# Cutting 1092 token columns as 512 + 512 + 68 in the dense products of a decoder-layer kernel

## Chip, cores and metric

One core of a Trainium2 chip. The metric is the device time in microseconds of one execution of the whole program, on inputs of fixed shape.

## What is computed

One layer of a hybrid decoder, on a prompt of 1024 tokens and on 8 sequences of 8 new tokens each, which makes 1088 tokens; all data is fp32. Cut to what matters:

```
def trunk_layer(x, ...):
    xn = rmsnorm(x, attn_norm_g)
    proj = xn @ w_in                                   # 1024 -> 3088
    gla_o  = gated linear attention, chunked           # 4 heads, 64/128
    diff_o = differential attention                    # 4 heads; 8 samples read a paged cache of 4096 tokens
    h = x + concat(norm(gla_o) * silu(gg), norm(diff_o)) @ w_out     # 1024 -> 1024
    hn = rmsnorm(h, ffn_norm_g)
    h = h + (silu(hn @ w_ffn_gate) * (hn @ w_ffn_up)) @ w_ffn_down   # 1024 -> 2816 -> 1024
    gate = sigmoid(rmsnorm(h, ple_norm_g) @ w_ple_gate)              # 1024 -> 1024
    return h + gate * (p @ w_ple_proj)                               # 256 -> 1024
```

## The kernel before

The activations stand transposed in SBUF: 128 features on the partitions, the tokens along the free dimension, `T = 3 * SPAN = 1092` columns (1088 tokens and four columns of padding, `SPAN = 364`). PSUM has 8 banks of 512 fp32 per partition. Two accumulators of three banks each, `dense[0]` (banks 0 to 2) and `dense[1]` (banks 3 to 5), take turns as the output of a dense product; two further banks, `misc`, take transposes and small products.

Every dense product is done by one helper, `product` (lines 143 to 156). It is given one tile of 128 output features and goes over the blocks of 128 input features (`ks`: 8 for an input width of 1024, 2 for an input width of 256). Weights and activations are each split into a high and a low part of type float32r (`whi`, `wlo`, `xhi`, `xlo`), and for each block three products are accumulated: high by high, high weight by low activation, low weight by high activation. Each of these three is cut along the token columns into three matmuls of 364 columns, `c` = 0, 1, 2, one to a bank (line 150). A matmul is at most 512 columns wide. Each of them is issued with a weight load of its own, although the three in a row use the same weights. After a block, `between` may put in other work of TensorE: transposes of an earlier tile (lines 435, 1832, 1854, 2319, 2329) or the sums of squares for the query and key norms (line 454).

The stages, in order of time:

- Input projection, line 425: 25 tiles of 8 blocks. ScalarE evacuates the accumulators (lines 367, 386, 392, 398, 404).
- Gated linear attention (lines 771 to 868), prompt attention (lines 1200 to 1224) and decode attention with its paged cache (lines 1448 to 1510). They don't call `product`. They hold plain fp32 matmuls and transposes of other shapes.
- Mixer output, line 1862: 8 tiles of 8 blocks; VectorE adds the result to h (line 1929).
- FFN, lines 2105 and 2114: 44 gate and up tiles of 8 blocks, scaled by VectorE (line 2146), and 11 times 8 down tiles of 2 blocks, added by VectorE (line 2167).
- Embedding, lines 2339 and 2348: 8 gate tiles of 8 blocks into `dense[0]` and 8 projection tiles of 2 blocks into `dense[1]`; VectorE evacuates both (lines 2402 and 2410). Line 2414 adds h.

Together 200 + 64 + 352 + 176 + 64 + 16 = 872 blocks.

The weights of a tile come by a DMA on SyncE's queue, GpSimd scales them by the norm's gain, ScalarE rounds them to the high part (`w_hi`, line 2051 in the FFN, 2283 in the embedding), and VectorE subtracts to get the low part (`w_lo`). All order between the engines is written out by hand with semaphores: TensorE waits for `w_lo` of the tile and for `evacuated` of the tile two before it (same accumulator), and counts up `product_done` with the tile's last matmul; the evacuating engine waits for that. The high part of a later tile waits for `product_done` too, as its buffer is reused.

The evacuations read an accumulator in its three spans, for which a view takes the first 364 of each bank's 512 elements, and `spans` (line 138) gives the SBUF side the same shape:

```
def spans(ap):
    return ap.rearrange("p (c n) -> p c n", n=SPAN)
...
dve.tensor_tensor(spans(m.h[:, n]), spans(m.h[:, n]), dense[n % 2][:, :, 0:SPAN], ALU.add
```

Of the kernel before, what the change touches and what calls it, by code (L numbers as in the profile page):

```python
# [15 lines left out]
ALU = mybir.AluOpType  # L16
ACT = mybir.ActivationFunctionType
# [8 lines left out]
SPAN = 364  # L26
T = 3 * SPAN
# [110 lines left out]
def spans(ap):  # L138

    return ap.rearrange("p (c n) -> p c n", n=SPAN)  # L140


def product(pe, out, whi, wlo, xhi, xlo, ks, between=()):

    for n, k in enumerate(ks):
        for w, x in ((whi, xhi), (whi, xlo), (wlo, xhi)):
            for c in range(3):
                ins = pe.matmul(out[:, c, 0:SPAN], w(k), x(k)[:, c * SPAN:c * SPAN + SPAN],  # L150
                                start=n == 0 and w is whi and x is xhi, stop=n == len(ks) - 1 and w is wlo)
        if n in dict(between):
            for work in dict(between)[n]:
                work()
    return ins


def input_projection(nc, io, m, ps, scr, sems):
# [21 lines left out]
    evacuated = sems("p1_evacuated")  # L180
# [15 lines left out]
    dense, misc = ps["dense"], ps["misc"]  # L196
# [22 lines left out]
    plan, n = {}, XT + 3 * 8  # L219
# [7 lines left out]
    with nc.Block() as block:  # L227
# [101 lines left out]
        def _(act):  # L329
# [17 lines left out]
            def hi(s, slot, first=False):  # L347
                act.wait_ge(w_scaled, s + 1)
                if not first:
                    act.wait_ge(product_done, s - 1)  # L350
                act.activation(m.whi[:, slot], m.raw[:, slot], ACT.Copy).then_inc(w_hi, 1)

            for g, (c0, cn) in enumerate(CHUNKS):
# [3 lines left out]
                for k in range(KT):  # L357
                    n = g * KT + k
# [3 lines left out]
            with act.Fori(0, 4) as i:  # L362
                for u in range(2):
                    s = 2 * i + u
                    act.wait_ge(product_done, s + 1)
                    act.wait_ge(filled, s * 3 + (XT - 3))
                    act.activation(spans(m.f[:, u]), dense[u][:, :, 0:SPAN], ACT.Copy).then_inc(evacuated, 1)
                    hi(s + 2, u)

            for s in range(8, 17):  # L370
                u, r = s % 2, s - 8
                if s >= 9:

                    v = 1 - u
                    act.wait_ge(taken, plan["ss", s - 1] + 3)
                    act.activation(m.rs[:, v], m.rs[:, v], ACT.Ln, scale=1.0 / DK, bias=m.eps[:, :]
                                   ).then_inc(ln_done, 1)
                    act.wait_ge(ln_done, s - 8)
                    act.activation(m.rs[:, v], m.rs[:, v], ACT.Exp, scale=-0.5).then_inc(rs_done, 1)
                act.wait_ge(product_done, s + 1)  # L380
                if s < 16:
                    if r < 2:
                        act.wait_ge(filled, XT + 3 * (s - 2) + 3)
                    else:
                        act.wait_ge(normed, r - 1)
                    act.activation(spans(m.f[:, u]), dense[u][:, :, 0:SPAN], ACT.Copy).then_inc(evacuated, 1)
                    act.wait_ge(evacuated, s + 1)
                    if r >= 2:
                        act.wait_ge(filled, plan["ss", s - 2] + 3)
                    act.activation(m.sq[:, u], m.f[:, u], ACT.Square).then_inc(squared, 1)  # L390
                else:
                    act.activation(spans(m.g[:, 0, :]), dense[0][:, :, 0:SPAN], ACT.Copy).then_inc(evacuated, 1)
                hi(s + 2, u)
            with act.Fori(0, 3) as i:
                for v in range(2):
                    s = 2 * i + (17 + v)
                    act.wait_ge(product_done, s + 1)
                    act.activation(m.g[:, bass.ds(2 * i + (1 + v), 1), :].rearrange("p o (c n) -> p (o c) n", n=SPAN),
                                   dense[1 - v][:, :, 0:SPAN], ACT.Copy).then_inc(evacuated, 1)
                    hi(s + 2, 1 - v)  # L400
            act.wait_ge(roped, 8)
            for s in (23, 24):
                act.wait_ge(product_done, s + 1)
                act.activation(spans(m.g[:, s - 16, :]), dense[s % 2][:, :, 0:SPAN], ACT.Copy).then_inc(evacuated, 1)

        @block.tensor
        def _(pe):
# [1317 lines left out]
def mixer(nc, io, m, ps, scr, sems):  # L1725
# [5 lines left out]
    s = {n: sems("p5_" + n) for n in names.split()}  # L1731
# [6 lines left out]
    dense, misc = ps["dense"], ps["misc"]  # L1738
# [7 lines left out]
    with nc.Block() as block:  # L1746
# [134 lines left out]
        def _(dve):  # L1881
# [29 lines left out]
            v = last.rearrange("p (h v) -> p h v", v=DV)  # L1911
# [14 lines left out]

            def evac(n):
                dve.wait_ge(s["product_done"], n + 1)
                dve.tensor_tensor(spans(m.h[:, n]), spans(m.h[:, n]), dense[n % 2][:, :, 0:SPAN], ALU.add
                                  ).then_inc(s["evacuated"], 1)  # L1930

            take_x(1, 16)
            evac(0)
            lo(2, 0)
            take_x(17, 24)
# [11 lines left out]
def ffn(nc, io, m, ps, scr, sems):  # L1947
# [11 lines left out]
    s = {n: sems("p6_" + n) for n in names.split()}  # L1959
# [4 lines left out]
    dense = ps["dense"]  # L1964
# [26 lines left out]
    with nc.Block() as block:  # L1991
# [142 lines left out]
        def _(dve):  # L2134
# [8 lines left out]
            def scaled(x, dst, bank):  # L2143

                dve.wait_ge(s["product_done"], x + 1)
                dve.tensor_tensor(spans(dst), dense[bank][:, :, 0:SPAN], spans(m.rb[:, :]), ALU.mult  # L2146
                                  ).then_inc(s["evacuated"], 1)

            def gate(j, f, x):
# [14 lines left out]

            def add(x, n):
                dve.wait_ge(s["product_done"], x + (n + 1))
                dve.tensor_tensor(spans(m.h[:, n]), spans(m.h[:, n]), dense[n % 2][:, :, 0:SPAN], ALU.add  # L2167
                                  ).then_inc(s["evacuated"], 1)

            lo(0, 0, 0)  # L2170
# [43 lines left out]
def embedding(nc, io, m, ps, scr, sems):  # L2214
# [5 lines left out]
    s = {n: sems("p7_" + n) for n in names.split()}  # L2220
    w_in = [sems(f"p7_w_in{u}") for u in range(2)]
    stored = [sems(f"p7_stored{u}") for u in range(2)]
    dense, misc = ps["dense"], ps["misc"]
# [6 lines left out]
    with nc.Block() as block:  # L2230
# [132 lines left out]
        def _(dve):  # L2363
# [34 lines left out]
            def scaled(n):  # L2398
                if not (isinstance(n, int) and n == 0):
                    dve.wait_ge(s["gated"], n)  # L2400
                dve.wait_ge(s["gate_done"], n + 1)
                dve.tensor_tensor(spans(m.gt), dense[0][:, :, 0:SPAN], spans(m.rb[:, :]), ALU.mult
                                  ).then_inc(s["gate_scaled"], 1)

            def result(n, u):
                dve.wait_ge(s["sigmoid_done"], n + 1)
                dve.wait_ge(s["proj_done"], n + 1)
                if not (isinstance(n, int) and n < 2):
                    dve.wait_ge(s["filled"], n * 3 + (PT - 3))
                dve.tensor_tensor(spans(m.gp[:, u]), spans(m.gt), dense[1][:, :, 0:SPAN], ALU.mult  # L2410
                                  ).then_inc(s["gated"], 1)
                dve.wait_ge(s["gated"], n + 1)
                h = m.h[:, bass.ds(n, 1), :].rearrange("p o t -> p (o t)")
                dve.tensor_tensor(m.gp[:, u], m.gp[:, u], h, ALU.add).then_inc(s["y_done"], 1)  # L2414
# [9 lines left out]
            with dve.Fori(0, 2) as i:  # L2424
                for u in range(2):
                    n = 2 * i + (2 + u)
# [112 lines left out]
```

## Time and profile before

| | us |
|---|---|
| timed executions, two | 2159.78 and 2168.81 |
| their median | 2164.3 |
| span of the profiled execution, first to last instruction | 2161.1 |
| TensorE busy with matmuls in the span | 1927.8 (89%) |
| TensorE busy with weight loads | 1743.4 (81%) |
| VectorE busy | 972.4 (45%) |
| ScalarE busy | 605.6 (28%) |
| GpSimd busy | 404.4 (19%) |

PE is TensorE's matmul side and PEld its weight loads, which overlap matmuls; DVE is VectorE, ACT ScalarE, POOL GpSimd, SP SyncE. The duration in a matmul's row runs from its start to the end of its results, so that the rows of neighbours overlap; the time between the starts of two matmuls is shorter than a row. Of a group of n records in a timeline the printed time runs from the first start to the last end. For the profiled execution only its span is known; what lies around it isn't listed separately.

### The profile page before, as it was taken

Reading aid. Unit: us, or ns where it says so; the run is one execution under the profiler, and the core shown is the slowest. Engines: PE = TensorE matmul, PEld = TensorE weight load, DVE = VectorE, ACT = ScalarE, POOL = GpSimd, SP = SyncE. Lnnn points to the kernel's source line nnn. Section 1 sums busy time; section 2 is a strip of 40 time slices with the busy share of each in tenths; the row PEclk is TensorE's granted clock in tenths of the full one; section 3 lists DMA queues with packets and bytes.
Section 4 is the critical chain, followed back from the end, with each engine's and each line's share of the span. In section 5 each row is a group of like instructions: output and inputs, shape, how many; then the busy total and the mean of one; then the engine's idle time right before and its main releaser. Section 6 shows DMA issues by size and latency. Waiting matters only on the chain. (4 is left out here: it accounts for less than half of the span.)

```text
span 2161.1 us, 36230 instructions
## 1 busy us (share of the span) xinstructions
PE 1927.8 (89%) x13348; PEld 1743.4 (81%) x13348; DVE 972.4 (45%) x1364; ACT 605.6 (28%) x1011; POOL 404.4 (19%) x398
## 2 busy tenths in 40 slices
PE   5999998556887789888789899999999999999798
PEld 4999998543555566656589899999999999999798
DVE  4224611784666545555533523433343334335543
ACT  4113312531444444444432211111111111112420
POOL 1112321331000234343311100110111011102210
PEclk9999999785878999999999999999999999999899
DMA  4323521005300799999721111111111111110221
GB/s 130 102 80 101 154 70 50 21 3 192 113 1 0 247 378 387 387 387 387 250 61 40 49 49 39 49 40 50 39 48 42 49 40 39 50 50 20 66 75 42
DMA packets 187844, 236.56 MB, mean 109 GB/s; under 512 B 12994, under 2 KB 127635, under 8 KB 187731
## 3 DMA queue, kind: packets, MB, share of 16 engines
q1 hardware_dynamic: 167250, 167.81, 24.3%
q0 software_dynamic: 20480, 67.13, 8.4%
q8 instruction: 85, 1.39, 0.3%
q14 instruction: 29, 0.23, 0.0%
HBM read 213.49 MB, written 16.92 MB: 107 GB/s over the span
## 5 line engine op out<-in xcount | busy, mean ns | idle before, releaser
L150 PE MATMUL psum<-h_hi,w_hi 128*128 128x364 f32 x1248 | 279.2, 332 | 2.5 <-issue 2.5
L150 PE MATMUL psum<-h_lo,w_hi 128*128 128x364 f32 x1248 | 276.6, 330 | 0.0
L150 PE MATMUL psum<-h_hi,w_lo 128*128 128x364 f32 x1248 | 275.4, 329 | 0.0
L2051 ACT ACTIVATE w_hi<-w_raw 128x1024 fp32r<-128x1024 f32 x66 | 68.9, 1060 | 584.4 <-PE psum L150 566.1
L150 PEld LDWEIGHTS psum<-h_hi,w_hi 128*128 128x128 f32 x1248 | 215.6, 189 | 4.6 <-issue 4.4
L150 PEld LDWEIGHTS psum<-h_lo,w_hi 128*128 128x128 f32 x1248 | 217.5, 189 | 0.0
L150 PEld LDWEIGHTS psum<-h_hi,w_lo 128*128 128x128 f32 x1248 | 217.1, 189 | 0.0
L2027 POOL TENSOR_TENSOR w_raw<-w_raw,gains 128x1024 f32<-128x1024 f32 x42 | 80.3, 1913 | 652.2 <-DMA w_raw<-in_w_ffn_gate 352.2
L150 PE MATMUL psum<-x_hi,w_hi 128*128 128x364 f32 x792 | 187.6, 345 | 11.1 <-DVE x_lo L1884 7.3
L1081 POOL DMA_DIRECT2D dec_v<-in_cache_v x256 | 138.0, 539 | 266.4 <-issue 263.3
L150 PE MATMUL psum<-x_hi,w_lo 128*128 128x364 f32 x792 | 176.4, 331 | 0.0
L150 PE MATMUL psum<-x_lo,w_hi 128*128 128x364 f32 x792 | 175.9, 330 | 0.0
L2167 DVE TENSOR_TENSOR h<-h,psum 128x1092 f32<-128x1092 f32 x88 | 113.5, 1290 | 108.1 <-PE psum L150 108.1
L1448 PE MATMUL psum<-consts,dec_k 128*128 128x128 f32 x1024 | 133.3, 286 | 31.3 <-DMA dec_k<-in_cache_k 23.1
L1448 PEld LDWEIGHTS psum<-consts,dec_k 128*128 128x128 f32 x1024 | 117.8, 147 | 51.0 <-issue 41.8
L150 PEld LDWEIGHTS psum<-x_hi,w_hi 128*128 128x128 f32 x792 | 136.5, 190 | 17.8 <-DVE x_lo L1884 7.5
L1380 ACT ACTIVATE dec_kt<-psum 128x512 f32<-128x512 f32 x192 | 101.7, 598 | 152.8 <-PE psum L1448 152.7
L150 PEld LDWEIGHTS psum<-x_lo,w_hi 128*128 128x128 f32 x792 | 138.9, 190 | 0.0
L150 PEld LDWEIGHTS psum<-x_hi,w_lo 128*128 128x128 f32 x792 | 138.7, 190 | 0.0
L2146 DVE TENSOR_TENSOR t_up<-psum,rstd_and_sum 128x1092 f32<-128x1092 f32 x22 | 28.5, 1296 | 207.7 <-PE psum L150 207.7
L150 PE MATMUL psum<-hidden_hi,w_hi 128*128 128x364 f32 x528 | 116.8, 329 | 2.5 <-DVE w_lo L2137 2.5
L150 PE MATMUL psum<-hidden_lo,w_hi 128*128 128x364 f32 x528 | 117.7, 331 | 0.0
(268 smaller groups left out, 2831.3 us busy)
## 6 DMA issues: line engine op xcount, KB each, us to landing
dec_v<-in_cache_v POOLq DMA_DIRECT2D x256, 256.0 KB, 5.7
dec_k<-in_cache_k SPq DMA_DIRECT2D x256, 256.0 KB, 8.8
w_raw<-in_w_in SPq DMA_DIRECT2D x25, 512.0 KB, 3.9
w_raw<-in_w_ffn_gate SPq DMA_DIRECT2D x22, 512.0 KB, 3.9
w_raw<-in_w_ffn_up SPq DMA_DIRECT2D x22, 512.0 KB, 3.8
w_raw<-in_w_ffn_down SPq DMA_DIRECT2D x22, 512.0 KB, 4.1
feat_swap<-feat_n SPq DMA_DIRECT2D x32, 136.5 KB, 2.4
x_in<-in_x_prompt SPq DMA_DIRECT2D x4, 1024.0 KB, 8.1
```

Of the source, the lines that this page charges most:

```text
L150: ins = pe.matmul(out[:, c, 0:SPAN], w(k), x(k)[:, c * SPAN:c * SPAN + SPAN], start=n == 0 and w is whi and x is xhi, stop=n == len(ks) - ...
L1081: eng.dma_start(ring[:, g % 4, p:p + 1, :], cache[bass.ds(page, 1)].rearrange("o t f -> t o f")).then_inc(sem[g % 4], 16)
L1380: act.activation(m.kt[:, g % 2, h, :], bank(h), ACT.Copy).then_inc(s["act_kt"], 1)
L1448: ins = pe.transpose(bank(h)[:, p * P:p * P + P], m.kr[:, g % 4, p, h * P:h * P + P], ident)
L2027: gp.tensor_tensor(m.raw[:, u], m.raw[:, u], gain(m, "ffn").unsqueeze(2).broadcast_to([P, KT, P]), ALU.mult).then_inc(s["w_scaled"], 1)
L2051: act.activation(m.whi[:, slot], m.raw[:, u], ACT.Copy).then_inc(s["w_hi"], 1)
L2146: dve.tensor_tensor(spans(dst), dense[bank][:, :, 0:SPAN], spans(m.rb[:, :]), ALU.mult).then_inc(s["evacuated"], 1)
L2167: dve.tensor_tensor(spans(m.h[:, n]), spans(m.h[:, n]), dense[n % 2][:, :, 0:SPAN], ALU.add).then_inc(s["evacuated"], 1)
```

## The change

`product` cuts the columns at 0, 512 and 1024 in place of 0, 364 and 728, and so fills the first two banks of an accumulator and 68 columns of the third. A view `flat` gives the accumulator as one run of 1092 elements across the three banks, and all evacuations of dense products read it and write flat SBUF rows. The other users of `SPAN` (the sums of squares in line 454, the low-rank gate in lines 697, 771 and 881, the norm sums in lines 1711 and 1719) stay with 364.

```diff
--- before.py
+++ after.py
@@ -140,14 +140,22 @@
     return ap.rearrange("p (c n) -> p c n", n=SPAN)
 
 
+CUTS = ((0, 512), (512, 512), (1024, T - 1024))
+
+
+def flat(banks):
+
+    return banks.rearrange("p c n -> p (c n)")[:, 0:T]
+
+
 def product(pe, out, whi, wlo, xhi, xlo, ks, between=()):
 
 
 
     for n, k in enumerate(ks):
         for w, x in ((whi, xhi), (whi, xlo), (wlo, xhi)):
-            for c in range(3):
-                ins = pe.matmul(out[:, c, 0:SPAN], w(k), x(k)[:, c * SPAN:c * SPAN + SPAN],
+            for a, n_cols in CUTS:
+                ins = pe.matmul(flat(out)[:, a:a + n_cols], w(k), x(k)[:, a:a + n_cols],
                                 start=n == 0 and w is whi and x is xhi, stop=n == len(ks) - 1 and w is wlo)
         if n in dict(between):
             for work in dict(between)[n]:
@@ -364,7 +372,7 @@
                     s = 2 * i + u
                     act.wait_ge(product_done, s + 1)
                     act.wait_ge(filled, s * 3 + (XT - 3))
-                    act.activation(spans(m.f[:, u]), dense[u][:, :, 0:SPAN], ACT.Copy).then_inc(evacuated, 1)
+                    act.activation(m.f[:, u], flat(dense[u]), ACT.Copy).then_inc(evacuated, 1)
                     hi(s + 2, u)
 
             for s in range(8, 17):
@@ -383,25 +391,25 @@
                         act.wait_ge(filled, XT + 3 * (s - 2) + 3)
                     else:
                         act.wait_ge(normed, r - 1)
-                    act.activation(spans(m.f[:, u]), dense[u][:, :, 0:SPAN], ACT.Copy).then_inc(evacuated, 1)
+                    act.activation(m.f[:, u], flat(dense[u]), ACT.Copy).then_inc(evacuated, 1)
                     act.wait_ge(evacuated, s + 1)
                     if r >= 2:
                         act.wait_ge(filled, plan["ss", s - 2] + 3)
                     act.activation(m.sq[:, u], m.f[:, u], ACT.Square).then_inc(squared, 1)
                 else:
-                    act.activation(spans(m.g[:, 0, :]), dense[0][:, :, 0:SPAN], ACT.Copy).then_inc(evacuated, 1)
+                    act.activation(m.g[:, 0, :], flat(dense[0]), ACT.Copy).then_inc(evacuated, 1)
                 hi(s + 2, u)
             with act.Fori(0, 3) as i:
                 for v in range(2):
                     s = 2 * i + (17 + v)
                     act.wait_ge(product_done, s + 1)
-                    act.activation(m.g[:, bass.ds(2 * i + (1 + v), 1), :].rearrange("p o (c n) -> p (o c) n", n=SPAN),
-                                   dense[1 - v][:, :, 0:SPAN], ACT.Copy).then_inc(evacuated, 1)
+                    act.activation(m.g[:, bass.ds(2 * i + (1 + v), 1), :].rearrange("p o t -> p (o t)"),
+                                   flat(dense[1 - v]), ACT.Copy).then_inc(evacuated, 1)
                     hi(s + 2, 1 - v)
             act.wait_ge(roped, 8)
             for s in (23, 24):
                 act.wait_ge(product_done, s + 1)
-                act.activation(spans(m.g[:, s - 16, :]), dense[s % 2][:, :, 0:SPAN], ACT.Copy).then_inc(evacuated, 1)
+                act.activation(m.g[:, s - 16, :], flat(dense[s % 2]), ACT.Copy).then_inc(evacuated, 1)
 
         @block.tensor
         def _(pe):
@@ -1926,7 +1934,7 @@
 
             def evac(n):
                 dve.wait_ge(s["product_done"], n + 1)
-                dve.tensor_tensor(spans(m.h[:, n]), spans(m.h[:, n]), dense[n % 2][:, :, 0:SPAN], ALU.add
+                dve.tensor_tensor(m.h[:, n], m.h[:, n], flat(dense[n % 2]), ALU.add
                                   ).then_inc(s["evacuated"], 1)
 
             take_x(1, 16)
@@ -2143,7 +2151,7 @@
             def scaled(x, dst, bank):
 
                 dve.wait_ge(s["product_done"], x + 1)
-                dve.tensor_tensor(spans(dst), dense[bank][:, :, 0:SPAN], spans(m.rb[:, :]), ALU.mult
+                dve.tensor_tensor(dst, flat(dense[bank]), m.rb[:, :], ALU.mult
                                   ).then_inc(s["evacuated"], 1)
 
             def gate(j, f, x):
@@ -2164,7 +2172,7 @@
 
             def add(x, n):
                 dve.wait_ge(s["product_done"], x + (n + 1))
-                dve.tensor_tensor(spans(m.h[:, n]), spans(m.h[:, n]), dense[n % 2][:, :, 0:SPAN], ALU.add
+                dve.tensor_tensor(m.h[:, n], m.h[:, n], flat(dense[n % 2]), ALU.add
                                   ).then_inc(s["evacuated"], 1)
 
             lo(0, 0, 0)
@@ -2399,7 +2407,7 @@
                 if not (isinstance(n, int) and n == 0):
                     dve.wait_ge(s["gated"], n)
                 dve.wait_ge(s["gate_done"], n + 1)
-                dve.tensor_tensor(spans(m.gt), dense[0][:, :, 0:SPAN], spans(m.rb[:, :]), ALU.mult
+                dve.tensor_tensor(m.gt, flat(dense[0]), m.rb[:, :], ALU.mult
                                   ).then_inc(s["gate_scaled"], 1)
 
             def result(n, u):
@@ -2407,7 +2415,7 @@
                 dve.wait_ge(s["proj_done"], n + 1)
                 if not (isinstance(n, int) and n < 2):
                     dve.wait_ge(s["filled"], n * 3 + (PT - 3))
-                dve.tensor_tensor(spans(m.gp[:, u]), spans(m.gt), dense[1][:, :, 0:SPAN], ALU.mult
+                dve.tensor_tensor(m.gp[:, u], m.gt, flat(dense[1]), ALU.mult
                                   ).then_inc(s["gated"], 1)
                 dve.wait_ge(s["gated"], n + 1)
                 h = m.h[:, bass.ds(n, 1), :].rearrange("p o t -> p (o t)")
```

## Rows read from the trace of the kernel before

**Rows 1.** The page's totals and its 40 slices, TensorE and its granted clock.

```profile
PE 1927.8 (89%) x13348; PEld 1743.4 (81%) x13348; DVE 972.4 (45%) x1364; ACT 605.6 (28%) x1011; POOL 404.4 (19%) x398
...
PE   5999998556887789888789899999999999999798
PEclk9999999785878999999999999999999999999899
```

**Rows 2.** Costliest groups: busy us, mean ns | idle before, releaser. Last: the embedding's small product.

```profile
L150 PE MATMUL psum<-h_hi,w_hi 128*128 128x364 f32 x1248 | 279.2, 332 | 2.5 <-issue 2.5
L150 PE MATMUL psum<-x_hi,w_hi 128*128 128x364 f32 x792 | 187.6, 345 | 11.1 <-DVE x_lo L1884 7.3
L150 PE MATMUL psum<-hidden_hi,w_hi 128*128 128x364 f32 x528 | 116.8, 329 | 2.5 <-DVE w_lo L2137 2.5
...
L150 PE MATMUL psum<-p_hi,w_proj_hi 128*128 128x364 f32 x48 | 10.5, 328 | 0.0
```

**Rows 3.** The chain that ended last: start us, us, what.

```profile
2066.26 10.49 PE psum L150 x63
```

**Rows 4.** Windows (length, PE and PEld busy, count, PEclk): line 150 in the FFN; input projection.

```profile
1230.00:1600.00 370.00, 369.03 (x2220) 368.73 (x2219) 1.00 0.15 45
...
39.00:310.00 271.00, 270.43 (x1607) 262.75 (x1607) 95.56 (x118) 67.73 (x65) 61.04 (x28) 0.99 0.36 99
```

**Rows 5.** Who waited for whom: us in total, times, longest.

```profile
ACT w_hi L2051 <- PE psum L150: 566.1, 49, 20.3
```

**Rows 6.** Timeline in the FFN: start us, us for the whole group, what.

```profile
1601.09 0.52 PEld L150 LDWEIGHTS psum<-hidden_hi,w_lo 128*128 128x128 f32 x3
1601.26 0.66 PE L150 MATMUL psum<-hidden_hi,w_lo 128*128 128x364 f32 x3
1601.59 0.52 PEld L150 LDWEIGHTS psum<-hidden_hi,w_hi 128*128 128x128 f32 x3
1601.76 0.65 PE L150 MATMUL psum<-hidden_hi,w_hi 128*128 128x364 f32 x3
```

**Rows 7.** Timeline of lines 1212 and 848; then durations (minimum/median/maximum).

```profile
557.28 1.41 PEld L1212 LDWEIGHTS psum<-att_v,att_wt 128*128 128x128 f32 x12 [0.76 <-issue]
470.60 1.72 PEld L848 LDWEIGHTS psum<-gla_s,gla_qblk 128*64 128x64 f32 x16 [0.17 <-issue]
...
L150 PEld LDWEIGHTS psum<-h_hi,w_hi x1248: 186/188/338, 1203.7 to 2146.1; 128*128 128x128 f32 x179
L1212 PEld LDWEIGHTS psum<-att_v,att_wt x288: 186/192/333, 528.2 to 705.9; 128*128 128x128 f32 x144
L1212 PE MATMUL psum<-att_v,att_wt x288: 275/275/583, 528.3 to 706.0; 128*128 128x128 f32 x144
L454 PE MATMUL psum<-feat_sq,consts x48: 467/469/573, 160.1 to 266.1; 128*128 128x364 f32 x48
L435 PEld LDWEIGHTS psum<-consts,feat x72: 111/140/142, 56.1 to 153.9; 128*128 128x128 f32 x64, 128*64 128x64 f32 x8
```

**Rows 8.** Timeline of weight loads where transposes of line 435 precede line 150.

```profile
82.42 0.47 PEld L150 LDWEIGHTS psum<-x_hi,w_hi 128*128 128x128 f32 x3
82.86 0.52 PEld L150 LDWEIGHTS psum<-x_lo,w_hi 128*128 128x128 f32 x3
```

**Rows 9.** Timelines: line 801 with 256 columns, line 454 with 364, plain fp32.

```profile
451.04 1.03 PE L801 MATMUL psum<-gla_v,gla_kds 128*128 128x256 f32 x4
160.11 0.78 PE L454 MATMUL psum<-feat_sq,consts 128*128 128x364 f32 x2
```

**Rows 10.** Groups of 1092 elements on VectorE and ScalarE.

```profile
L2414 DVE TENSOR_TENSOR ple_gate_and_y<-ple_gate_and_y,h 128x1092 f32<-128x1092 f32 x8 | 10.4, 1296 | 0.7
L2402 DVE TENSOR_TENSOR ple_gate_and_y<-psum,rstd_and_sum 128x1092 f32<-128x1092 f32 x8 | 10.4, 1296 | 7.7 <-PE psum L150 7.7
L390 ACT ACTIVATE feat_sq<-feat 128x1092 f32<-128x1092 f32 x8 | 9.0, 1123 | 0.3
L386 ACT ACTIVATE feat<-psum 128x1092 f32<-128x1092 f32 x8 | 8.7, 1086 | 36.1 <-PE psum L150 36.1
```

## The prediction

> **What bounds the kernel now.** First the page's totals: TensorE is busy 89% of the span, the next engine (VectorE) 45%, and in the 40 slices PE reads 9 in slices 2 to 6 and nearly throughout from slice 24 to 38, with a granted clock of 9 tenths there [rows 1]. The forms of line 150 say what it does: groups of 1248, 792, 528 and 48 matmuls of 128x364, each of them there for three pairs of operands, so 3 x 2616 = 7848 matmuls, every one with a weight load of its own [rows 2]. 7848 matmuls in threes over the column pieces are 2616 triples, and the change acts on each triple.
>
> How long is one matmul really? Not the 329 to 345 ns of its rows, which overlap. The chain of waits has an unbroken run of 63 of them in 10.49 us, 166.5 ns from one to the next [rows 3], so a triple takes 499.5 ns. The busy shares by stage agree: 2220 in 370 us in the middle of the FFN, none of it idle to speak of, and PE is busy 270 of 271 us in the input projection [rows 4]. In total 7848 x 166.5 ns = 1307 us, 60% of the span, lie in this one line, and little hides them: everything that waits, waits for it, and it waits for others 16 us in all (11.1 + 2.5 + 2.5) [rows 2]. So what a triple gains or loses goes nearly one for one into the time.
>
> **What sets the 166.5 ns.** At the granted clock of 1.00, the upper level of 2.4 GHz, 364 columns stream in 151.7 ns. 14.8 ns are left over. The timeline shows three loads from 1601.09 on and the three matmuls they serve from 1601.26 on, so the third of these starts at 1601.59; the next three loads start at 1601.59 as well, and their matmuls at 1601.76. A load starts when the matmul before its own starts, never earlier, and has that matmul's time to run under [rows 6]. So only one load runs ahead, and one matmul must take at least as long as one load.
>
> How long is a load? Line 1212 (plain fp32, 128x128 weights, 128 columns) has 12 loads in 1.41 us: (1.41 - 0.19) / 11 = 111 ns from one to the next. Line 848 has the same 128 columns but half-width weights, and 16 of its loads take 1.72 us; with a last one as short as a transpose's, 0.14 us, that is (1.72 - 0.14) / 15 = 105 ns, so there the load binds less. The loads of line 150 read 188 ns, those of line 1212 192 [rows 7]. The best witness is a place where line 150 follows short transposes: three of its loads fit in 0.47 us where they otherwise take 0.52 [rows 8]. Of 0.47 - 0.19 = 0.28 us, one interval of 166.5 is normal, and 114 ns remain for the first, which followed a short matmul: that is the load of line 150's own kind, exposed.
>
> **The change part by part.** It removes nothing from the count: three matmuls and three loads per triple, before and after, and 1092 columns in both. It moves columns: two pieces of 512 and one of 68.
>
> *The two long pieces.* No row has this operand type at 512 columns. From the durations of the plain fp32 rows, which make two passes per record: 275 ns at 128 columns and 469 at 364, so (469 - 275) / 236 = 0.822 ns a column [rows 7], half of it, 0.411 ns, in one pass. Then a long piece takes 166.5 + 148 x 0.411 = 227.3 ns. If instead the 14.8 ns grow with the columns it is 166.5 x 512 / 364 = 234.2. If they vanish in a longer stream it is 216: line 801 streams 256 columns twice, the same 512 column times, and starts four matmuls in 1.03 us, (1.03 - 0.38) / 3 = 216 ns [rows 9]. I take 228, next to the slope, which comes from the nearest rows.
>
> *The short piece.* Its columns need 68 / 2.4 = 28 ns, or 166.5 - 296 x 0.411 = 45 ns by the slope, but its successor's load starts only when it starts, and takes 111 to 114 ns. From below it is 111 ns, from above 128 ns: that is, if a short piece streamed at the four passes that plain fp32 takes (line 1212 has 288 records for 144 products, each of two passes), 68 x 4 / 2.4 = 113, plus the 14.8. I take 113.
>
> *Sum.* 2 x 228 + 113 = 569.0 ns against 499.5: +69.5 ns a triple, x 2616 = +181.8 us. In other words TensorE's gain is 3 x 166.5 - (2 x 228 + 45) = about nothing on the columns, and the loss is the 68 ns that it stands idle under each short piece.
>
> *Taken off.* Where transposes follow a triple (some 80 places, three to a turned tile), the load behind the short piece is a transpose's, 140 ns where line 150's reads 188, so about 50 ns shorter [rows 7]: -4 us. Where TensorE waits for operands anyway (the 16 us of [rows 2], mostly where a stage begins), longer triples fill the wait: -7 us, between 0 and -16. Net +171 us.
>
> *The evacuations.* They read the same 1092 elements, now in one run across three banks. VectorE takes 1296 ns for line 2402, which reads PSUM in three spans, and 1296 for line 2414, which is flat and in SBUF; ScalarE 1086 for PSUM in spans and 1123 for flat SBUF [rows 10]. I count 0, with 0.04 us either way; each lies under the next tile's product, except the last ones, 2 x 1.3 us at the end. Were they uncovered, 0.04 us on each of the 181 (25 + 8 + 44 + 88 + 16) would be 7 us. Loads, scaling and splitting of weights only get more slack: ScalarE's rounding of weights in the FFN waits 566 us on this line already [rows 5].
>
> The profiled execution's span is 2161.1 us, between the two timed runs (2159.8 and 2168.8) and 3.2 under their median; nothing around the span is known separately, so I add the difference to the median: 2164.3 + 171 = 2335 us.
>
> The Trainium skill (TensorE: Matmul & The Clock Gate, section Back-to-back issue gap) puts the spacing at N/2.4 + 2.5 ns, 154 ns for 364 columns, where the trace has 166.5; the measurement decides. By its formula for 512, 215.8, and its section on LDWEIGHTS (columns / 1.2, 106.7 ns, near the 111 of line 1212) a triple would be 538 ns, +39 ns over today's, an estimate of +101 us.
>
> **The rivals.**
> - *The surplus grows with the columns.* 2 x 234.2 + 113 = 581.4, +81.9 ns, x 2616 = 214, less 11: 2367 us. For it: 14.8 ns could be a slower rate. Against: the slope of the plain rows.
> - *The surplus vanishes in a long piece.* 2 x 216 + 113 = 545, +45.5 ns, 119 - 11: 2272 us. For it: line 801's 216. Against: plain fp32 never shows the surplus, not at 364 columns either (line 454, 0.78 - 0.47 = 0.31 us for two passes of 151.7) [rows 9], so that row is of another kind.
> - *The short piece is worse than its load*, four passes and the surplus: 2 x 228 + 128 = 584, +84.5 ns, 221 - 11: 2374 us. No row speaks for or against.
> - *No change.* Loads run ahead by more than one, so that the short piece costs its 45 ns: 2 x 227.3 + 45 = 499.6, nothing. 2164 us. Against it: the load starts of [rows 6] and the 114 ns of [rows 8]. The same page of the Trainium skill (section Step-by-step: what each phase is for) says that TensorE pulls weight loads ahead of matmuls in flight when they go to the background buffer; the trace agrees for one load, and no row shows two.
> - *Faster.* Loads run ahead and the surplus goes with the long stream: 2 x 216 + 45 = 477, -22.5 ns, -59 us: 2105 us. The place is the hand-over from the short piece to the next 512; the time falls below today's from the point where the short piece costs less than 499.5 - 432 = 67.5 ns, and the rows put it at 111 or more.
>
> **How the numbers follow.** Forecast (load-bound short piece, long piece near 228) 0.62; surplus proportional 0.15; surplus gone 0.08; short piece slower 0.07; no change 0.05; faster 0.03. The range runs from the lowest load-bound case, 2 x 216 + 111 = 543, +114 us, less all 16 us of waits and the 4, 2258 us, to the highest, 2 x 234.2 + 128 = 596.4, +96.9 ns or +253 us with nothing hidden, 2418. A measurement of this kernel tells about 2% from no change: faster 0.03, within 2% 0.05, slower 0.92.
>
> **What would show it.** In the profile after, the matmul line has 5232 matmuls of 128x512 and 2616 of 128x68. In a timeline of the FFN, a 68 is followed by the next start after 111 to 114 ns, a 512 after about 228, and a run of 21 triples takes 11.9 us instead of 10.5. The PE digits fall in the dense stages while the waits of ScalarE and VectorE on line 150 grow by the same third of a microsecond for every five triples; line 2402 stays at 1.3 us. Attention and the gated-linear part keep their lengths. The forecast is wrong if the start after a 68 comes within 70 ns, if the 512s stand closer than 220 or wider than 236 ns, or if the granted clock falls in the FFN, which today holds 1.00 while TensorE is never idle and would then be idle 12% of the time.

## The result and the profile after

The kernel after takes 2359.5 us (median of two, 2356.8 to 2362.1) against 2164.3: ratio 1.091, 95% interval 1.088 to 1.094. It is slower by 195 us. The profiled execution's span is 2355.2 us, 194.1 us over that of before.

The page's totals and slices of the kernel after, to set beside [rows 1]:

```profile
PE 2130.9 (90%) x13348; PEld 1716.0 (73%) x13348; DVE 968.3 (41%) x1364; ACT 606.0 (26%) x1011; POOL 402.7 (17%) x398
...
PE   5999999556887798887999999999999999999898
...
PEclk8999999785878999999899999999999999999999
```

TensorE is busy 203 us longer and the other engines about as long as before (VectorE 968 us against 972). The granted clock reads 9 tenths nearly throughout the dense slices in both kernels, and 1.00 in the FFN window below as in [rows 4], so the clock is not where the time went.

The dense line is now line 158 and has the two forms; the first row answers to the 1248 of [rows 2], split into 832 and 416. Columns: busy us, mean ns, idle before.

```profile
L158 PE MATMUL psum<-h_hi,w_hi 128*128 128x512 f32 x832 | 296.3, 437 | 1.0 <-issue 0.9
...
L158 PE MATMUL psum<-h_hi,w_hi 128*128 128x68 f32 x416 | 81.1, 195 | 0.0
...
L158 PE MATMUL psum<-p_hi,w_proj_hi 128*128 128x68 f32 x16 | 3.1, 194 | 0.0
```

A stretch of the FFN and the chain of waits, as in [rows 4] and [rows 3]:

```profile
1290.00:1690.00 400.00, 399.72 (x2083) 338.03 (x2082) 1.00 0.13 39
```

```profile
2248.87 12.02 PE psum L158 x63
```

2083 matmuls in 400 us are 576.1 ns a triple, where 2220 in 370 us were 500.0. In this window matmuls are again never idle by their own rows (399.72 of 400 us), but PEld, which was busy 368.73 of 370 us, is busy 338 of 400: there is room between the loads now. The run of 63 matmuls takes 12.02 us, not 10.49.

Where the time came in shows in the first and last start of the lines that bound the stages. The line of the low-rank gate comes right behind the input projection, and the last line of the decode attention right before the mixer. Kernel before, columns as in [rows 7] (minimum/median/maximum ns, first and last start):

```profile
L771 PE MATMUL psum<-gla_in,small x12: 464/464/540, 370.0 to 373.5; 16*128 16x364 f32 x12
```

```profile
L1510 PE MATMUL psum<-dec_osc,consts x16: 272/297/421, 793.0 to 1066.0; 128*32 128x128 f32 x16
```

The same two lines in the kernel after:

```profile
L779 PE MATMUL psum<-gla_in,small x12: 464/464/540, 414.1 to 417.5; 16*128 16x364 f32 x12
```

```profile
L1518 PE MATMUL psum<-dec_osc,consts x16: 272/297/421, 837.8 to 1112.0; 128*32 128x128 f32 x16
```

Up to the gate the kernel after loses 44.1 us (414.1 - 370.0), over 600 triples, 73.5 ns each. From there to the end of decode attention, where no dense product stands, it is 697.9 against 696.0 us: 2 us. From there to the end it is 1243.2 against 1095.1 us, +148 us over 2016 triples, 73.5 ns each. So the loss lies in the dense products alone, evenly by their number.

A timeline as in [rows 6], two products in the FFN of the kernel after:

```profile
1500.53 0.53 PEld L158 LDWEIGHTS psum<-h_hi,w_lo 128*128 128x128 f32 x3
1500.56 0.74 PE L158 MATMUL psum<-h_hi,w_lo 128*128 128x512 f32 x3
1501.11 0.53 PEld L158 LDWEIGHTS psum<-h_hi,w_hi 128*128 128x128 f32 x3
1501.13 0.71 PE L158 MATMUL psum<-h_hi,w_hi 128*128 128x512 f32 x2
```

A narrow window shows what overlaps at 1500.7 us, a short piece and the first long piece behind it:

```profile
1500.53 0.19 PE L158 MATMUL psum<-h_lo,w_hi 128*128 128x68 f32 x1
1500.53 0.30 PEld L158 LDWEIGHTS psum<-h_hi,w_lo 128*128 128x128 f32 x2
1500.56 0.48 PE L158 MATMUL psum<-h_hi,w_lo 128*128 128x512 f32 x1
```

And one at 1501.04 us, the second long piece and the load of the short piece behind it:

```profile
1500.87 0.40 PE L158 MATMUL psum<-h_hi,w_lo 128*128 128x512 f32 x1
1500.87 0.19 PEld L158 LDWEIGHTS psum<-h_hi,w_lo 128*128 128x128 f32 x1
```

The three loads of a pair of operands serve its 512, 512 and 68 columns. The first starts when the short matmul before it starts (1500.53), the second 0.30 - 0.19 = 0.11 us later, a whole load's time, and the third when the second 512 starts (1500.87). The record of the first 512 begins already 0.03 us behind the short one's, while its own load is still running, and is 0.48 us long in place of 0.40: the time that TensorE loses lies inside this record and not in front of it. So the busy share does not show the loss, and the starts of matmuls put it in the wrong place: 0.03 us behind the 68, 0.31 us from the first 512 to the second. The starts of the loads show it. Group to group it is 1501.11 - 1500.53 = 0.58 us: 0.11 us for the short piece with its exposed load, and the remaining 0.47 us for the two long pieces.

### The profile page after: what moved, and what is told of

Its sections match the earlier page's. It is cut to its first block and busy times, and to the rows that moved or that the text cites. A ratio compares the mean times of both kernels' runs of the same rounds, so it can differ in the third digit from the quotient of the medians.

```text
span 2355.2 us, 36230 instructions
## 1 busy us (share of the span) xinstructions
PE 2130.9 (90%) x13348; PEld 1716.0 (73%) x13348; DVE 968.3 (41%) x1364; ACT 606.0 (26%) x1011; POOL 402.7 (17%) x398
## 5 line engine op out<-in xcount | busy, mean ns | idle before, releaser
L158 PE MATMUL psum<-h_hi,w_hi 128*128 128x512 f32 (+1 forms) x1248 | 309.9, 356 | 1.0 <-issue 0.9
L158 PE MATMUL psum<-h_hi,w_lo 128*128 128x512 f32 (+1 forms) x1248 | 308.5, 355 | 0.0
L158 PE MATMUL psum<-h_lo,w_hi 128*128 128x512 f32 (+1 forms) x1248 | 306.9, 354 | 0.0
L2059 ACT ACTIVATE w_hi<-w_raw 128x1024 fp32r<-128x1024 f32 x66 | 68.7, 1057 | 693.7 <-PE psum L158 681.8
L158 PEld LDWEIGHTS psum<-h_lo,w_hi 128*128 128x128 f32 x1248 | 203.6, 190 | 37.4
L158 PEld LDWEIGHTS psum<-h_hi,w_lo 128*128 128x128 f32 x1248 | 203.2, 189 | 36.4
L158 PE MATMUL psum<-x_hi,w_hi 128*128 128x512 f32 (+1 forms) x792 | 203.0, 365 | 10.0 <-DVE x_lo L1892 6.2
L158 PE MATMUL psum<-x_lo,w_hi 128*128 128x512 f32 (+1 forms) x792 | 198.0, 358 | 0.0
L158 PE MATMUL psum<-x_hi,w_lo 128*128 128x512 f32 (+1 forms) x792 | 196.9, 357 | 0.0
L158 PE MATMUL psum<-hidden_hi,w_hi 128*128 128x512 f32 x528 | 131.0, 356 | 2.5 <-DVE w_lo L2145 2.5
L158 PE MATMUL psum<-hidden_hi,w_lo 128*128 128x512 f32 x528 | 130.9, 356 | 0.0
```

The costliest lines, as they stand in the source:

```text
L158: ins = pe.matmul(flat(out)[:, a:a + n_cols], w(k), x(k)[:, a:a + n_cols], start=n == 0 and w is whi and x is xhi, stop=n == len(ks) - 1 a ...
L2059: act.activation(m.whi[:, slot], m.raw[:, u], ACT.Copy).then_inc(s["w_hi"], 1)
```

## The experiments

Where no interval is given, a time below is one execution, beside the kernel before on the same chip (2165.3 us in experiments 1 to 8, 2163.1 in 9 to 11). 22 executions of the kernel before, timed beside experiments 5 to 8, lie between 2159.5 and 2170.4 us, so a difference of some 5 us between two such times, or 2 ns a triple, says nothing by itself. Theory L: each float32r matmul takes the longer of its own stream and one weight load of about 109 ns.

**1. A third piece of 232 columns.**

```diff
-CUTS = ((0, 512), (512, 512), (1024, T - 1024))
+CUTS = ((0, 0, 512), (512, 512, 512), (1024, T - 232, 232))
...
-            for a, n_cols in CUTS:
-                ins = pe.matmul(flat(out)[:, a:a + n_cols], w(k), x(k)[:, a:a + n_cols],
+            for o, a, n_cols in CUTS:
+                ins = pe.matmul(out.rearrange("p c n -> p (c n)")[:, o:o + n_cols], w(k), x(k)[:, a:a + n_cols],
```

> Third piece of 232 columns in place of 68 (columns 860 to 1091, written to the start of the third bank, so the outputs of the last 68 columns are not the reference's). Theory L: a matmul takes the longer of 0.457 ns a column and one weight load, 109 ns. 232 columns stream in 106 ns, under the load, so the 164 extra columns are free: 2359 us, within 6. Rival S: a matmul costs a fixed 78 ns plus its columns (78 + 31 = 109 for 68): then 184 ns, +75 ns a triple, +196 us, 2555 us. Rival Q: a piece under 256 columns streams in four passes (68 x 4 / 2.4 = 113): then 387 ns, +278 ns a triple, +727 us, 3086 us.

Measured 2359.2 us, where the kernel after took 2359.5; that they agree so closely is chance, within the scatter they are equal. 164 more columns in each of 2616 matmuls cost nothing. The window and the form of the third piece (mean ns in the second row):

```profile
1290.00:1690.00 400.00, 399.88 (x2082) 337.91 (x2081) 1.00 0.13 39
```

```profile
L158 PE MATMUL psum<-h_hi,w_hi 128*128 128x232 f32 x416 | 111.8, 269 | 0.0
```

2082 matmuls in 400 us, where the kernel after had 2083. Its records are longer (269 against 195 ns), their spacing is not. Rivals S (a fixed cost and the columns) and Q (four passes for a short piece) are out, by 196 and 727 us.

**2. A third piece of 364 columns.** The same edit with 364 for 232.

> Third piece of 364 columns in place of 68 (outputs of the last 68 columns not the reference's). L: above the load, 0.457 x 364 = 166.4 ns, +57 ns a triple x 2616 = +150 us over the 68: 2509 us, span near 2505. S: 78 + 166 = 244 ns, +135 ns, +353 us, 2712 us. Q: 364 is over 256, one pass, the same 2509 as L. If the 14.8 ns over the clock rate were a fixed cost of each matmul and 512 takes its 233.7 for another reason, the 364 still takes 166.4, so this run also checks that 166.4 holds next to 512s.

Measured 2498.3 us: +139 us over the kernel after, where L gave +150 and S +353.

```profile
1700.00:2000.00 300.00, 299.94 (x1427) 257.42 (x1426) 1.00 0.11 34
```

300 us over 1427 matmuls are 630.7 ns a triple. Above the load the columns count again.

**3. No third piece.** The last 68 token columns are not computed.

```diff
-CUTS = ((0, 512), (512, 512), (1024, T - 1024))
+CUTS = ((0, 512), (512, 512))
```

> The 68-column piece is left out (the last 68 token columns are not computed). L: the triple loses a whole load time, 576.6 to 467.4 ns, -109.2 x 2616 = -286 us: 2073 us, faster than the kernel before by about 4%. If the short piece only cost its columns, 31 ns, and the rest of the loss lay in the 512-column pieces: -81 us, 2278 us.

Measured 2070.3 us: -289 us from the kernel after, -110.6 ns a triple, for 28 ns' worth of columns at 2.4 GHz. This is the short piece's price, taken out alone.

```profile
1250.00:1600.00 350.00, 350.00 (x1513) 283.80 (x1512) 1.00 0.16 48
```

It also gives the long piece by itself: 1513 in 350 us, 231.3 ns. Then the triple of experiment 2 is 2 x 231.3 + 168.1, close to the 166.5 of before, and the kernel after's 576.1 is 2 x 231.3 + 113.5.

**4. The short piece in the middle.**

```diff
-CUTS = ((0, 512), (512, 512), (1024, T - 1024))
+CUTS = ((0, 512), (1024, T - 1024), (512, 512))
```

> The same three pieces in the order 512, 68, 512. L: the load that is exposed is the one behind the short piece wherever it stands: 2359 us, within 6; where transposes follow a triple, their shorter load (about 50 ns) no longer stands behind the short piece, some 80 places, +4 us. If the loss were at the change from one weight block to the next (the short piece stands there now), it would go with the order: up to -78 ns a triple, -200 us, 2160 us.

Measured 2354.0 us, 5.5 us under the kernel after: within 6 of 2359, though not with the +4 us written down beside it. The loss does not sit at the change from one weight block to the next, for which 2160 us stood. A difference of 5 us is within the scatter, and its cause was not followed.

**5. Six pieces of 182.** The kernel before with each piece cut in two. Two matmuls now write to one bank in turn; only the first carries the start flag and only the second the stop flag, and the result stays the same.

```diff
-            for c in range(3):
-                ins = pe.matmul(out[:, c, 0:SPAN], w(k), x(k)[:, c * SPAN:c * SPAN + SPAN],
-                                start=n == 0 and w is whi and x is xhi, stop=n == len(ks) - 1 and w is wlo)
+            for c, a in ((0, 0), (0, 182), (1, 0), (1, 182), (2, 0), (2, 182)):
+                ins = pe.matmul(out[:, c, a:a + 182], w(k), x(k)[:, c * SPAN + a:c * SPAN + a + 182],
+                                start=n == 0 and w is whi and x is xhi and a == 0, stop=n == len(ks) - 1 and w is wlo and a != 0)
```

> The kernel before with each 364-column piece cut in two of 182, six matmuls and six loads for each pair of operands; the result is the same. L: 182 columns stream in 83 ns, the load takes 109, so six times 109.2 = 655 ns in place of 499.3, +156 ns x 2616 = +408 us: 2572 us. If only very short pieces expose their load, or loads run further ahead: 6 x 83 = 499, no change, 2164 us. With a fixed 14.8 ns for each matmul and free loads: +3 x 14.8 = +44 ns, +116 us, 2280 us.

Measured 3270.0 us, far from every number written down. The clock row of the page and two windows of the FFN (the third figure from the right is the granted clock) say why:

```profile
PEclk6999997687999989999995555555555555555599
```

```profile
1380.00:1720.00 340.00, 338.33 (x3030) 338.17 (x3030) 1.00 0.11 32
1740.00:3090.00 1350.00, 1335.86 (x6261) 1334.74 (x6260) 0.50 0.06 18
```

At the upper level, 2.4 GHz, 3030 matmuls take 340 us: 112.2 ns each, the load's time that L gave (109). At the lower level, 1.2 GHz, 6261 take 1350 us: 215.6 ns, where 182 columns stream in 151.7. So the load binds at both levels, and takes 1.92 times as long at half the clock. The sum closes: 15,696 matmuls at 112.2 ns are 1761 us, 454 over the 1307 of before; 6369 of them fall in the 1368 us of the lower level, at 103.4 ns more each, another 659; 2165 + 454 + 659 = 3278 against 3270. L's part is borne out, and a clock that nobody had in the sum costs more than the part under test.

**6. A 512 cut into 256 + 256.**

```diff
-CUTS = ((0, 512), (512, 512), (1024, T - 1024))
+CUTS = ((0, 256), (256, 256), (512, 512), (1024, T - 1024))
...
-                                start=n == 0 and w is whi and x is xhi, stop=n == len(ks) - 1 and w is wlo)
+                                start=n == 0 and w is whi and x is xhi and a != 256, stop=n == len(ks) - 1 and w is wlo and a != 0)
```

> The kernel after with its first piece of 512 cut into 256 + 256; the result is the same. L with a rate of 0.457 ns a column: 256 takes 117 ns, above the load's 109, so the two take 234 and nothing changes: 2359 us. If the surplus over the clock rate were fixed for each matmul (20 ns at 512): 2 x (106.7 + 20) = 253, +20 ns a triple, +52 us, 2411 us. If it is fixed at 14.8 as at 364: +9 ns, +24 us.

Measured 2377.4 us, +18 us or 6.9 ns a triple. Neither purely proportional (0) nor purely fixed (+24 or +52), and nearer to the fixed 14.8. A window of the FFN agrees, 583.1 ns for four matmuls (2058 in 300 us) where the kernel after had 576.1 for three:

```profile
1300.00:1600.00 300.00, 298.56 (x2058) 275.52 (x2058) 1.00 0.13 39
```

The two 256s together take 231.3 + 6.9 = 238.2, so 119 ns each, still over the load. The surplus over 2.4 GHz is then 12.4 ns at 256 columns, 14.8 at 364 and 18.0 at 512: about 7 ns and 0.022 ns a column. Each rests on one or two executions, so these last digits are rough.

**7. The evacuations alone.** The matmuls of the kernel before under the evacuations of the kernel after, which here read columns that no product writes, where a bank is filled to 364 only, and leave out as many that one does.

```diff
-            for a, n_cols in CUTS:
-                ins = pe.matmul(flat(out)[:, a:a + n_cols], w(k), x(k)[:, a:a + n_cols],
+            for c in range(3):
+                ins = pe.matmul(out[:, c, 0:SPAN], w(k), x(k)[:, c * SPAN:c * SPAN + SPAN],
```

> The matmuls of the kernel before (364 columns, one to a bank) with the evacuations of the kernel after, which read 1092 elements in one run across the banks (so they take stale columns and the outputs are not the reference's). The evacuations cost nothing in either theory: 2164 us, ratio to before 1.000 within 0.003. If they carried part of the loss: up to 8 us (181 of them at 0.04 us).

Measured 2164.5 us beside 2165.3, ratio 0.9999, interval 0.9988 to 1.001. The second part of the change costs nothing. In the kernel after, VectorE's flat evacuation and the flat sum in SBUF read, as in [rows 10]:

```profile
L2422 DVE TENSOR_TENSOR ple_gate_and_y<-ple_gate_and_y,h 128x1092 f32<-128x1092 f32 x8 | 10.4, 1296 | 0.7
L2410 DVE TENSOR_TENSOR ple_gate_and_y<-psum,rstd_and_sum 128x1092 f32<-128x1092 f32 x8 | 10.4, 1296 | 8.9 <-PE psum L158 8.9
```

**8. Without the padding columns.** The kernel before with 364, 364 and 360.

```diff
-            for c in range(3):
-                ins = pe.matmul(out[:, c, 0:SPAN], w(k), x(k)[:, c * SPAN:c * SPAN + SPAN],
+            for c, n_cols in enumerate((SPAN, SPAN, SPAN - 4)):
+                ins = pe.matmul(out[:, c, 0:n_cols], w(k), x(k)[:, c * SPAN:c * SPAN + n_cols],
```

> The kernel before with pieces of 364, 364 and 360: the four padding columns are no longer computed, the 1088 tokens are. L with 0.457 ns a column: -4 x 0.457 = -1.8 ns a triple x 2616 = -4.8 us: 2159.5 us, ratio 0.998. If a matmul's time goes in coarser steps than a column, or other limits hold: 0.

Measured 2160.5 us beside 2165.3, ratio 0.9977, interval 0.9965 to 0.9989: -4.8 us. This version beats both kernels, by little. Four columns in 1092 are seen, because each piece is above the load's time.

**9. Two short pieces.** The kernel after with 34 + 34 for 68.

```diff
-CUTS = ((0, 512), (512, 512), (1024, T - 1024))
+CUTS = ((0, 512), (512, 512), (1024, 34), (1058, 34))
...
-                                start=n == 0 and w is whi and x is xhi, stop=n == len(ks) - 1 and w is wlo)
+                                start=n == 0 and w is whi and x is xhi and a != 1058, stop=n == len(ks) - 1 and w is wlo and a != 1024)
```

> The kernel after with its piece of 68 cut into 34 + 34; the result is the same. L: each exposes a whole load, 109.2 ns, although it streams in 15: +109.2 x 2616 = +286 us over the kernel after, 2645 us, if the granted clock stays at its upper level. TensorE then streams 455 of 686 ns (1092 columns at 2.4 GHz), 66%. The six pieces of 182 streamed 455 of 673 ns, 68%, at the upper level, and the clock fell to 1.2 GHz for 1368 us of their FFN. If it is the share of time without columns that the clock follows, it falls here too, for hundreds of microseconds, and the time is well over 2700 us (a triple at 1.2 GHz is 2 x 427 + 2 x 213 = 1280 ns; all of it there: up to +1300 us). If the fall came from the shape or count of the pieces, the clock stays and it is 2645.

Measured 2653.8 us: +294 us over the kernel after, 112.5 ns for a second matmul on the same 68 columns. That is the load's time once more. The clock stayed at its upper level but for moments (one of 7 us is shown under experiment 11):

```profile
PEclk8999999685888999989999999999999999999999
```

```profile
1700.00:2000.00 300.00, 298.20 (x1738) 260.30 (x1738) 1.00 0.11 32
```

Columns stream for 66% of the time here, with the clock at 1.00, and for 68% in experiment 5 before it fell; that share alone does not explain the fall.

**10. One of three pieces cut in two.** The kernel before with 182, 182, 364 and 364.

```diff
-            for c in range(3):
-                ins = pe.matmul(out[:, c, 0:SPAN], w(k), x(k)[:, c * SPAN:c * SPAN + SPAN],
-                                start=n == 0 and w is whi and x is xhi, stop=n == len(ks) - 1 and w is wlo)
+            for c, a, b in ((0, 0, 182), (0, 182, 364), (1, 0, 364), (2, 0, 364)):
+                ins = pe.matmul(out[:, c, a:b], w(k), x(k)[:, c * SPAN + a:c * SPAN + b],
+                                start=n == 0 and w is whi and x is xhi and a == 0, stop=n == len(ks) - 1 and w is wlo and b == 364)
```

> The kernel before with only the first of its three pieces cut into 182 + 182; the result is the same. L: 2 x 112 (the interval of the 182s at the upper clock level) + 2 x 166.4 = 557 ns, +57.5 ns x 2616 = +150 us: 2315 us. 455 of 557 ns stream, 82%, more than the 79% of the kernel after, which kept its clock, so it stays here too. If two short pieces in a row are what lowers the clock, it is well above 2350.

Measured 2310.6 us, against 2315. Two pieces under the load in a row don't keep the clock low by themselves:

```profile
1700.00:1950.00 250.00, 247.42 (x1782) 246.83 (x1781) 1.00 0.13 39
```

**11. The six pieces of 182 again.**

> The six pieces of 182 once more, now also timed in a round. If the lower clock is this kernel's own doing, it falls again in the FFN and the times are again far above 2618 us (15,696 matmuls at the 112.2 ns of the upper level, +454 us); where it falls may move, and the time with it, by hundreds of microseconds. If the first look met a disturbed chip: 2618 us.

Measured 3269.5 us (3266.3 and 3272.7), ratio 1.511, interval 1.507 to 1.515. The clock row of the page falls in the same slice as in experiment 5:

```profile
PEclk7999997678999989999995555555555555555699
```

It is the kernel's own behaviour and repeats to a few us. What TensorE did before the clock fell is the same in both: it had waited for VectorE's sum into h, 1.67 us in experiment 5 and 1.78 in experiment 11 (first and second line), the longest wait since the FFN's beginning. The clock is at 0.50 from 1720 us on, and back at 1.00 only from 3089 us, behind the end of the FFN (third line, experiment 5):

```profile
1719.19 0.91 PE L150 MATMUL psum<-h_hi,w_hi 128*128 128x182 f32 x6 [1.67 <-DVE h L2167]
```

```profile
1715.77 1.09 PE L150 MATMUL psum<-h_hi,w_hi 128*128 128x182 f32 x6 [1.78 <-DVE h L2167]
```

```profile
1720.00:3089.00 1369.00, 1358.46 (x6353) 1355.41 (x6352) 220.39 (x174) 96.90 (x92) 69.93 (x35) 0.50 0.06 19
```

A fall behind a wait is nothing special. In experiment 9 TensorE waits 2.52 us in the FFN, the clock reads 0.52 for 7 us and then 1.00 again:

```profile
2418.50 1.46 PE L158 MATMUL psum<-hidden_hi,w_hi 128*128 128x512 f32 x4 [2.52 <-DVE w_lo L2145]
```

```profile
2418.00:2425.00 7.00, 6.50 (x21) 5.53 (x22) 0.52 0.26 77
2425.00:2450.00 25.00, 25.00 (x148) 21.91 (x147) 1.00 0.00 1
```

What sets the six pieces of 182 apart is that the clock does not come back: not for 1369 us in the FFN, and not for 37 us at the beginning of the input projection (41 to 78 us), where the kernel before is back at 1.00 from 43 us on:

```profile
41.00:78.00 37.00, 36.88 (x173) 36.64 (x172) 0.50 0.06 15
```

Why it does not stays open, and that the wait of 1.7 us is what started the fall is read from two executions and not tested. Experiments 9 and 10 had waits of 2.52 us in their FFN and came back, so neither the streaming share nor two short pieces in a row is enough by itself.

## Why the prediction was right, and which term was off

**The direction and the mechanism.** The forecast was 2335 us (range 2258 to 2418), the result 2359.5. The step that carries it, that a short piece exposes a whole weight load, is shown from four sides: widening it to 232 columns is free (1), leaving it out gives back 110.6 ns a triple (3), cutting it in two costs 112.5 ns (9), and at half the clock the spacing of load-bound matmuls grows to 1.92 times (5). Predicted were 113 ns; 576.1 - 2 x 231.3 leaves 113.5. The witness in [rows 8], one exposed load behind short transposes, had the right size. The two terms that were off (below) err the same way and don't cancel, so the number did not come out by luck.

**The signs named beforehand** were in part badly chosen, and by their letter they speak against a forecast that was right. It was to be wrong "if the start after a 68 comes within 70 ns, if the 512s stand closer than 220 or wider than 236 ns". By the matmuls' records the start after a 68 comes after 0.03 us, and the two 512s stand 0.31 us apart; only the starts of the loads give 0.11 us behind the 68 and 0.47 for the two 512s, or 0.23 to 0.24 each. The PE digits were to fall in the dense stages, and don't: matmuls are busy 399.72 of 400 us, because the wait for the load lies inside the next record. It is PEld that falls, from 368.73 of 370 to 338.03 of 400 us. The 63 matmuls in a row were to take 11.9 us and took 12.02.

**The long piece was mis-sized.** This is the term that was most off. The prediction put it "at 228, next to the slope" of the plain fp32 rows. Alone it measured 231.3 ns (3). With it the triple is 2 x 231.3 + 113.5 = 576.1 in place of 569.0, +7.1 ns x 2616 = +19 us of the 24 us by which the forecast was low. Half the slope of plain fp32, 0.411 ns a column (even a little under the 0.417 of 2.4 GHz), is not the slope of float32r: between 364 and 512 columns it is (231.3 - 166.5) / 148 = 0.438. The plain rows never showed the surplus over the clock rate, which the prediction itself held against the rival at 216 and should have held against borrowing their slope too. The truth lies between the forecast's long piece and the rival "surplus grows with the columns" (234.2, 2367 us), about halfway. As stated, that rival is excluded by experiment 6, where two 256s cost 6.9 ns more than one 512.

**What was taken off.** The two FFN windows give 576.1 - 500.0 = 76.1 ns, x 2616 = 199 us. The dense stages grew by 44.1 + 148.1 = 192 us, so 7 us were hidden in them, not 11 (and 2 us came in outside, between the gate and the mixer). The waits of TensorE at the beginnings of stages hardly shrank. The costliest of the groups has an idle of 10.0 us where [rows 2] had 11.1, with the same releaser:

```profile
L158 PE MATMUL psum<-x_hi,w_hi 128*128 128x512 f32 (+1 forms) x792 | 203.0, 365 | 10.0 <-DVE x_lo L1892 6.2 <-DVE w_lo L1903 3.3 <-DVE x_lo L510 0.6
```

With the 1.0 and 2.5 us of the other two groups it is 13.5 us where it was 16.1, so -7 us for these waits was too much; they gave 2.6. The -4 us for loads of transposes behind a short piece is borne out by the trace. Three of these loads, right behind a 68 in the kernel after:

```profile
59.56 0.31 PEld L443 LDWEIGHTS psum<-consts,feat 128*128 128x128 f32 x3
59.84 0.19 PEld L158 LDWEIGHTS psum<-x_hi,w_hi 128*128 128x128 f32 x1
```

From the third to the next load, behind a transpose, it is 59.84 - (59.56 + 0.31 - 0.14) = 0.11 us, and the same from the second to the third; of 0.31 - 0.14 = 0.17 us between the first and the third, 0.06 us remain for the one behind the 68. That is 0.05 us less than line 158's own load, about 4 us in some 80 places.

**The evacuations** cost nothing, as predicted (7), and the engines behind TensorE only waited longer: ScalarE's rounding of weights waits 681.8 us on the dense line, where [rows 5] had 566.1.

```profile
ACT w_hi L2059 <- PE psum L158: 681.8, 50, 24.0
```

**The other rivals.** No change and faster both needed loads that run ahead by more than one. Experiment 3's price of 110.6 ns for 68 columns excludes them. The timeline after has exactly one load ahead, which starts with the matmul before its own or, behind a short piece, when the load before it gives way, 0.11 us after that one's start. The Trainium skill (TensorE: Matmul & The Clock Gate, section Step-by-step: what each phase is for) says that TensorE pulls weight loads ahead of matmuls in flight; the trace agrees for that one load. A long piece hides one load completely, and the time left over is not carried to the next: the load at 1500.87 starts with the second 512, and not earlier. The surplus that vanishes (216) is out by the 231.3, and the short piece in four passes by experiment 1. The estimate of +101 us, made of 215.8 ns for a long piece and 106.7 for a load, is out by the measured 231.3 and 113.5 ns.

**The clock** reads 1.00 in the FFN windows of the kernel after (0.943 on average over the span, as before), with columns streaming 79% of a triple's time, so the caveat of the prediction did not come true here. Experiment 5 shows that it was worth writing down.

## What to carry to other kernels

When every matmul carries its own weight load, cost each piece as the longer of its stream and one load, and cut evenly. For float32r weights of 128x128 the load is 109 to 113 ns at the upper clock, which is what some 230 columns take to stream; a shorter piece pays for columns that it doesn't use. (A plain fp32 record streams each column twice [rows 9], so 230 is not its number.) Filling a bank to its 512 columns brings little (one matmul more cost 7 ns in experiment 6, and here the count stayed the same), while the remainder of 68 costs a whole load. Read the exposed load from the starts of neighbouring loads behind a short matmul, and not from the busy share, the durations of the rows or the starts of the matmuls, none of which shows it.

## What the runs showed of the hardware

- A piece of 232 columns costs what one of 68 costs (2359.2 against 2359.5 us), and 68 cut in two pieces of 34 cost one load more, 112.5 ns.
- The record of a matmul can begin before its weight load has ended: a 512 behind a 68 begins 0.03 us after its load and is 0.48 us long in place of 0.40.
- float32r matmuls with 128x128 weights follow each other at 119 ns for 256 columns, 166.5 for 364 and 231.3 for 512, 12 to 18 ns more than their columns take at 2.4 GHz, where a plain fp32 record at 364 columns, two passes in 0.31 us, showed no such surplus [rows 9]. The cause was not looked for.
- The interval of load-bound matmuls follows the granted clock: 112.2 ns at 1.00 and 215.6 ns at 0.50.
- With six pieces of 182 columns the clock fell to its lower level behind a wait of 1.7 us and stayed there for 1369 us, in both executions; with two of 34 beside two of 512, and a smaller share of streaming, it fell behind a wait of 2.52 us and was back 7 us later. The fall cost 659 us, more than the 454 us of exposed loads.
